# A hybrid decoder step on one core: the samples' rows between out-projection and experts, and the end of the last expert pair

## The reference, cut to what matters

```python
n = rmsnorm(h, norm_mix);  u = n @ w_in              # z | xBC | dt | q | k | v
y_ssd = ssd_branch(...)                               # conv, SiLU, Mamba-2 scan, gate, grouped norm
o     = dilated attention, merged, rmsnorm
h = h + concat(y_ssd, o) @ w_out                      # out-projection
x = rmsnorm(h, norm_ffn)
logits = x @ router_w + router_b                      # 32 experts
top_val, top_idx = top_k(logits, 4); gates = softmax(top_val)
for every token and each of its 4 experts e:
    hcat = x @ w1[e] + b1[e]                          # 1024 -> 2048
    g = min(glu, 7) * sigmoid(1.702 * min(glu, 7)) * (clip(lin, -7, 7) + 1)
    h += gate * (g @ w2[e] + b2[e])                   # 1024 -> 1024
y = rmsnorm(h, norm_final)
```

## Time and profile before

| what | value |
|---|---|
| median of 3 runs | 1234.51 us (1234.47 to 1235.19) |
| the profiled execution in all | 1238.29 us |
| its span | 1236.5 us |
| PE, DVE, ACT, POOL busy | 1155.0, 364.6, 230.2, 55.2 us |
| read from HBM, over the span | 455.82 MB, 375 GB/s |
| loads of experts, time from issue to landing | 37 to 39 us |

### The profile page before, as it was taken

One profiled execution on the slowest core, in us unless ns is written; L12 is line 12 of the kernel. 1 busy time (PEld: TensorE's weight loads), 2 busy tenths in 40 slices (PEclk: granted clock), 3 DMA queues, 4 the chain that ended last, 5 costly groups with the idle time before them and its releaser, 6 DMA issues.

```text
span 1236.5 us, 15869 instructions
## 1 busy us (share of the span) xinstructions
PE 1155.0 (93%) x6400; PEld 527.0 (43%) x6400; DVE 364.6 (29%) x749; ACT 230.2 (19%) x464; POOL 55.2 (4%) x49
## 2 busy tenths in 40 slices
PE   9999999899999999999989898989898989898897
PEld 7777666435443443434333332424242323232332
DVE  2467336764512130221213030303021121212122
ACT  2013453624501101111010101010111011010103
POOL 0000033530000000000000000000000000000000
PEclk9999999999899999999999999999999999999999
DMA  9677567479599999999999999999999999999996
GB/s 292 206 259 250 201 198 283 139 274 416 241 427 426 429 426 429 427 429 428 429 427 429 427 429 428 429 427 429 427 429 428 429 429 428 429 427 429 427 427 252
DMA packets 64368, 463.58 MB, mean 375 GB/s; under 512 B 7704, under 2 KB 25268, under 8 KB 38380
## 3 DMA queue, kind: packets, MB, share of 16 engines
q1 hardware_dynamic: 62206, 459.02, 90.2%
q10 hardware_dynamic: 1582, 2.22, 0.5%
q0 software_dynamic: 544, 1.84, 0.4%
HBM read 455.82 MB, written 7.24 MB: 375 GB/s over the span
## 4 chain that ended last, share of the span: by engine, by line
PE 57%; DMA 37%; DVE 2%; ACT 2%; issue 2%; SPq 0%; POOL 0%; ACTq 0%; DVEq 0%; POOLq 0%
DMA ring<-in_w 34%; PE ps L2399 21%; PE ps L1883 10%; PE ps L2423 5%; DMA own<-in_w 3%; PE ps L2331 2%; PE ps L2323 2%; PE ps L2291 2%; PE ps L2325 1%; PE ps L2168 1%; PE ps L1925 1%; PE ps L2342 1%; PE ps L2385 1%; PE ps L2210 1%; PE ps L1959 1%
## 5 line engine op out<-in xcount | busy, mean ns | idle before, releaser
L2399 PE MATMUL ps<-ring,own 128*64 128x512 f32 x1456 | 326.9, 595 | 29.6 <-DMA ring<-in_w 29.6
L1728 DVE TENSOR_SCALAR own<-ps 128x512 f32<-128x512 f32 x32 | 22.1, 692 | 678.9 <-PE ps L2399 678.7
L2399 PEld LDWEIGHTS ps<-ring,own 128*64 128x64 f32 x1456 | 104.1, 137 | 235.0 <-issue 178.9
L2423 PE MATMUL ps<-ring,own 128*64 128x512 f32 x592 | 133.5, 594 | 14.1 <-ACT own L1130 13.9
L2399 PE MATMUL ps<-own 128*64 128x512 f32 x592 | 134.1, 594 | 11.4 <-DMA own<-in_w 11.4
L1883 PE MATMUL ps<-own,ring 128*128 128x288 f32 x512 | 129.9, 409 | 0.0
L1883 PEld LDWEIGHTS ps<-own,ring 128*128 128x128 f32 x512 | 95.1, 190 | 28.8 <-issue 4.4
L2423 PE MATMUL ps<-own 128*64 128x512 f32 x432 | 98.4, 595 | 8.3 <-ACT own L1130 7.0
L2399 PEld LDWEIGHTS ps<-own 128*64 128x64 f32 x592 | 43.1, 137 | 94.7 <-issue 84.5
L2423 PEld LDWEIGHTS ps<-ring,own 128*64 128x64 f32 x592 | 44.1, 137 | 90.0 <-issue 70.3
L1130 ACT ACTIVATE own<-ps 64x512 f32<-64x512 f32 x60 | 35.5, 592 | 245.2 <-PE ps L2423 244.4
(11 more groups left out here) (378 smaller groups left out, 985.9 us busy)
## 6 DMA issues: line engine op xcount, KB each, us to landing
ring<-in_w SPq DMA_DIRECT2D x128, 2048.0 KB, 38.5
own<-in_w SPq DMA_DIRECT2D x63, 2048.0 KB, 37.4
ring<-in_w_in SPq DMA_DIRECT2D x16, 1024.0 KB, 7.8
ring<-in_cache_win_k SPq DMA_DIRECT2D x8, 1024.0 KB, 5.5
ring<-in_cache_win_v SPq DMA_DIRECT2D x8, 1024.0 KB, 4.8
ring<-in_w_out SPq DMA_DIRECT2D x6, 1024.0 KB, 10.9
ring<-in_state_ssm SPq DMA_DIRECT2D x8, 512.0 KB, 6.9
out_ssm_sample<-ring SPq DMA_DIRECT2D x8, 512.0 KB, 8.9
```

Source lines behind the costliest of these rows:

```text
L1728: nc.vector.tensor_scalar(xg_o, hid[:, 0], LIMIT, None, ALU.min).then_inc(sem("glu_ready"), 1)
L2399: last = nc.tensor.matmul(ps[C * half:C * half + C, 1 + m, :], xT[:, k, C * u:C * u + C], rows[:, D * half + 512 * m:D * half + 512 * m + ...
L2423: last = nc.tensor.matmul(ps[C * half:C * half + C, 4, :], gT[:, (k % 4) * P + C * (k // 4):(k % 4) * P + C * (k // 4) + C], rows[:, 512 * ...
```

## The change

- Between out-projection and experts, the samples: their three bf16 parts are now made right after their norm, ahead of the norm of tile 1, into `first_parts` (the room of `gT`, not yet in use). `first_places` writes the samples' selection three times, into 96 bf16 rows `S1s`. `first_samples` gathers them with eight bf16 products of 96 rows in place of `gather_tile(2, 1)`, in one go, after the turn of tile 1's second half; the openings follow the first half of tile 1's router instead of standing ahead of it. Tile 0's gather is cut after its first column block instead of in the middle. Later, ACT copies `first_parts` to `sample_parts`. `XN_PARTS` becomes 15.
- The end: in the last pair `second` of the first expert opens tile 1's banks at step 0, and tile 2's at step 4, where the second expert's turn now stands too; its columns go to a buffer of their own, `gT_last`. On ACT the copy of the first expert's rows (`closing_rows(pt, 0)`) comes after those columns and the last sums. After the second expert PE adds tile 1's first rows before it waits for the second rows, then tile 0's, tile 2's first, and the rest.
- The last units: 9 and 10 are loaded in two halves each, 11 in four quarters, each with a semaphore, and `second` waits for a piece when it comes to it.

```diff
+        S1s = sub(r_xbcP, 2 * 2 * C, C).bitcast(BF16)
+        first_parts = gT.bitcast(BF16)
-        XN_PARTS = 14
+        XN_PARTS = 15
+        gT_last = sub(r_xnT, D + TOK, 512)
+        END_ROWS = {9: (0, 2), 10: (0, 2), 11: (0, 1, 2, 3)}
+        def end_full(n, row):
+            return unit_full(n % UNITS) if row == 0 else sem(f"end_rows{n}_{row}")
...
@@ SP, last pair
-                if n < PER_PAIR - 1:
+                if n not in END_ROWS:
                     unit_load(NE - 2, n)
-            (two halves of the last unit, the second with sem("end_rows"))
+                    continue
+                of, _, j = pair_unit(n)
+                for row, end in zip(END_ROWS[n], END_ROWS[n][1:] + (W2_ROWS,)):
+                    sp.dma_start(unit(n % UNITS)[:, D * row:D * end], w2[NE - 2 + of, j][:, D * row:D * end]).then_inc(end_full(n, row), 16)
...
@@ ACT
+            act.wait_ge(sem("mixT_ps"), len(MIX_TURNS))
+            act.wait_ge(sem("xn_ready"), 2)
+            nc.scalar.activation(samples[NS:2 * NS], samples[0:NS], ACT.Copy)
+            rounded(samples[2 * NS:3 * NS], samples[0:NS], 2, 0)
+            rounded(first_parts[0:96], samples[0:96], 3, 0)
+            rounded(first_parts[NS:2 * NS], samples[NS:2 * NS], 4, 1)
+            rounded(first_parts[2 * NS:3 * NS], samples[2 * NS:3 * NS], 5, 1)
+            rounded(first_parts[2 * NS:3 * NS], samples[2 * NS:3 * NS], 6, 2)
             norm_tile(1, 2)
             normed_tile(1, 2)
             gate_exp(1, 2)
...
             act.wait_ge(sem("xT_ps"), 2)
-            nc.scalar.activation(samples[NS:2 * NS], samples[0:NS], ACT.Copy)
-            rounded(samples[2 * NS:3 * NS], samples[0:NS], 3, 0)
-            rounded(sample_parts[0:96], samples[0:96], 4, 0)
+            rounded(sample_parts[0:96], first_parts[0:96], 8, 0)
             for c in range(2):
-                rounded(token_parts[c][0], xn[:, c, :], 5 + c, 0)
-            rounded(sample_parts[NS:2 * NS], samples[NS:2 * NS], 7, 1)
-            rounded(sample_parts[2 * NS:3 * NS], samples[2 * NS:3 * NS], 8, 1)
-            rounded(sample_parts[2 * NS:3 * NS], samples[2 * NS:3 * NS], 9, 4)
+                rounded(token_parts[c][0], xn[:, c, :], 9 + c, 0)
...
@@ ACT, closing_turn
                 sums_to_banks(1)
-                closing_rows(pt, 0)
-                hidden_columns(2 * pt + 1)
+                hidden_columns(2 * pt + 1, gT_last)
                 act.wait_ge(sem("turned_ps"), 5)
                 sums_to_banks(2)
+                closing_rows(pt, 0)
...
@@ DVE, first_places
+                targets = [S1s[NS * r:NS * r + NS] for r in range(3)] if c == 2 else [S1[:, c]]
+                for to in targets:
+                    last = (the selection, built into `to`)
+                last.then_inc(sem("S_ready"), 1)
...
@@ DVE
+            left_over(xn[0:96, 2, :], first_parts[0:96], 4)
             add_mixed(1, 0)
+            dve.wait_ge(sem("xn_left"), 1)
+            left_over(xn[64:96, 2, :], first_parts[64:96], 6)
             tokens_to_lanes(1, 0, 4)
             add_mixed(1, 1)
             tokens_to_lanes(1, 1, 5)
...
@@ PE
+            def first_samples():
+                pe.wait_ge(sem("xn_ready"), 7)
+                pe.wait_ge(sem("S_ready"), 2)
+                for k in range(KT):
+                    nc.tensor.matmul(ps[:, FIRST_BANKS[k // 4], P * (k % 4):P * (k % 4) + P], first_parts[0:96, lane_columns(k)], S1s[0:96], start=False, stop=False)
...
+            half_scored()
             pe.wait_ge(zeroed, 6)
             pe.wait_ge(sem("b1_parts"), 6)
             for bank in FIRST_BANKS:
                 nc.tensor.matmul(ps[:, bank, :], zeros, b1p[0:1, 0:512], start=True, stop=False)
-            gather_tile(2, 1, (0,))
-            half_scored()
             pe.wait_ge(sem("h_mixed"), 5)
             h_turn(1, 1)
-            gather_tile(2, 1, (1,))
+            first_samples()
             pe.wait_ge(sem("xnT_dve"), 13)
             router(1, range(4, KT))
-            gather_tile(0, 0, (0,))
+            first_tile(0, 0, 1, range(1))
             router_sum(1, 2)
-            gather_tile(0, 0, (1,))
+            first_tile(0, 0, 1, range(1, KT))
             prefix(1, 2)
...
-            gather_tile(1, 2)
+            first_tile(1, 2, 8, range(KT))
...
@@ PE, second
-                        if ending and n == PER_PAIR - 1 and k % W2_ROWS == 2:
-                            pe.wait_ge(sem("end_rows"), 16)
+                        if ending and k % W2_ROWS in END_ROWS.get(n, ())[1:]:
+                            pe.wait_ge(end_full(n, k % W2_ROWS), 16)
...
-                    second(pt, 0, first, {4: open_rest} if closing else {})
-                    pe.wait_ge(sem("gT_ready"), 2 * pt + 1)
-                    hidden_turn(pt, 1)
+                    second(pt, 0, first, {0: open_next, 4: open_last_and_turn} if closing else {})
+                    if not closing:
+                        pe.wait_ge(sem("gT_ready"), 2 * pt + 1)
+                        hidden_turn(pt, 1)
...
+            pe.wait_ge(sem("read_act"), 4)
+            add_closing(1, 0)
             pe.wait_ge(sem("ysb_ready"), more * (4 * PASS_STEP * PAIRS) + (4 * PAIRS + 1))
+            add_closing(0, 1).then_inc(sem("comb_ps"), 1)
+            pe.wait_ge(sem("read_act"), 5)
+            add_closing(2, 0)
+            for c in range(1, 3):
                 add_closing(c, 1).then_inc(sem("comb_ps"), 1)
```

More of the change, by code:

```diff
@@ L1083, in _, with rounded @@
             nc.scalar.activation(stat[:, 61:62], stat[:, 60:61], ACT.Sqrt)
+            def rounded(to, source, rounds, left):
+                act.wait_ge(sem("xn_ready"), rounds)
+                if left:
+                    act.wait_ge(sem("xn_left"), left)
+                nc.scalar.activation(to, source, ACT.Copy).then_inc(sem("xn_ready"), 1)
+            samples = xn[:, 2, :]
+            act.wait_ge(sem("mixT_ps"), len(MIX_TURNS))
[6 more added lines that the diff above has]
+            rounded(first_parts[2 * NS:3 * NS], samples[2 * NS:3 * NS], 6, 2)
             norm_tile(1, 2)
@@ L1739, in _ @@
             dve.wait_ge(sem("gate_ready"), 3)
-            for rows, tiles in ((P, slice(0, 2)), (NS, slice(2, 3))):
-                _, weights, _, s1, s2 = pair_views(0, rows, tiles, S1)
-                nc.vector.tensor_tensor(s2, s1, weights, ALU.mult).then_inc(sem("S_ready"), 1)
+            _, weights, _, s1, s2 = pair_views(0, P, slice(0, 2), S1)
+            nc.vector.tensor_tensor(s2, s1, weights, ALU.mult).then_inc(sem("S_ready"), 1)
+            nc.vector.tensor_tensor(S2[0:NS, 2].rearrange("p (u c) -> p u c", u=2), S1s[0:NS].rearrange("p (u c) -> p u c", u=2),
+                                    gate[0:NS, 2, 0:2].unsqueeze(2).broadcast_to([NS, 2, C]), ALU.mult).then_inc(sem("S_ready"), 1)
             for r in range(1, 3):
@@ L2202, in lane_columns, with first_tile @@
                 return slice(start, start + W1_ROWS * (P - 1) + 1, W1_ROWS)
-            def gather_tile(c, s, halves=(0, 1)):
-                n = ROWS[c]
-                pe.wait_ge(sem("xn_ready"), s + 1)
+            def first_tile(c, s, ready, ks):
+                pe.wait_ge(sem("xn_ready"), ready)
                 pe.wait_ge(sem("S_ready"), s + 1)
-                for half in halves:
-                    for j in range(4):
-                        last = nc.tensor.matmul(ps[:, FIRST_BANKS[half], P * j:P * j + P], xn[0:n, c, lane_columns(4 * half + j)], S1[0:n, c, :], start=False, stop=(c == 1 and j == 3))
-                    if c == 1:
+                for k in ks:
+                    last = nc.tensor.matmul(ps[:, FIRST_BANKS[k // 4], P * (k % 4):P * (k % 4) + P], xn[:, c, lane_columns(k)], S1[:, c, :], start=False, stop=(c == 1 and k % 4 == 3))
+                    if c == 1 and k % 4 == 3:
                         last.then_inc(sem("xT_ps"), 1)
+            def first_samples():
[3 more added lines that the diff above has]
+                    nc.tensor.matmul(ps[:, FIRST_BANKS[k // 4], P * (k % 4):P * (k % 4) + P], first_parts[0:96, lane_columns(k)], S1s[0:96], start=False, stop=False)
             natural = list(range(12))
```

47 lines of the change are left out of this document (17 added, 30 removed).

## The result

The change made the kernel slower: 1240.86 us, median of 7 (1239.35 to 1241.37), against 1235.72 us (1234.47 to 1237.49) of the kernel before on the same chip; ratio 1.0032, interval 1.0017 to 1.0047. The profiled execution of after took 1241.37 us with a span of 1239.6. The forecast was 1229.2, and the range ended at 1234.4.

The account below looks back on a forecast made before the run. The expert weights' DMA stream sets the pace over most of the span, with gains only before and after it; head 5.1 plus tail 0.2 makes 5.3 us off 1234.51, so 1229.2 us, range 1227.0 to 1234.4.

Parts of the forecast that it names:

- The ground: Head to last landing: each microsecond the first expert starts earlier moves the whole weights' stream, and so the end, forward.
- A: Head: the granted clock stays high; gain 3.7 to 6.6 us, 5.1 taken, 1229.2 us with the tail; chance 0.50.
- B: Head: the clock falls all the same; gain 0.7 to 1.4 us, 1.1 taken, 1233.2 us with the tail; chance 0.40.
- the 32-row lots: Head: the samples' 32-row products ahead of the clock's fall become 96-row matmuls, an argument for A; no size of its own.
- The size of the head: Head up to the first expert: 5.1 us gained, the middle of A's 3.7 to 6.6.
- A's far end: Head: the high clock holds to the end of the low stretch, a gain of 6.6 us.
- C: Head: roundings and subtractions on ACT and DVE at twice their price come 5.6 us late for PE; 1238.8 us, chance 0.06.
- The tail: From the ninth unit to the end: together a gain of 0.2 us, bounds 0.5 gain and 0.2 loss.
- The first openings: Tail: two openings (0.5 us) move to where PE idled 1.30 us, but wait for DVE's read, so hidden or not.
- the 0.19 us of the wait for unit 10: Tail: PE's 0.19 us wait goes, since the turn comes ahead of the last half of unit 9.
- the four records: Tail after the second expert: four closing-sum records (0.94 us) move under a 0.76 us wait; 0.15 to 0.75 us kept.
- D: Tail: each of eight load pieces costs 0.4 us more than its bytes, 3.2 us using up slack and gain; 1235, chance 0.04.

Follow-up runs that it names:

- the shifted after: Changed kernel with three of six warm-up products written as 24 small ones, so its expert loop begins at 4080, not 4044: 1234.61 us, ratio 0.9989.
- past the limit: Kernel before with all six warm-up products written as 48 small ones, so its loop spans 4133 to 5863: 1246.30 us, ratio 1.0087.
- the control: Kernel before with the same 36 added warm-up instructions, loop from 4097 to 5827: 1237.26 us, ratio 1.0016.
- the two halves: Kernel before with only PE's new head order (1236.87 us, ratio 1.0003), and with only the new bf16 sample parts in the old order (1236.14 us, ratio 0.9993).
- three more traces of the old head: Kernel before with 36 or 72 more instructions ahead of the loop, or eleven idle products each turn: head stretch 14.1, 14.3 and 13.0 us.

## Why the prediction was wrong

- **The ground: "Each microsecond by which this start comes forward moves the whole stream forward, up to the last landing".** This step failed. The stream did start with the first unit's release, 5.1 us earlier, as the prediction's last paragraph asked, but it did not keep its pace: 830.6 us for 822.8. The prediction counted instructions that went away on PE only as time at the head; that 17 fewer of them move the code behind them was not in it. No rival covered it. The term that is missing is worth 7.6 to 7.9 us on the stream, and in the totals 6.3 us (after against the shifted after, two sessions) to 9.0 (past the limit against the control, 2.2 of it ahead of the loop). Against the kernel before on the same chip the forecast was 10.4 us off: the stream 7.8, the head 3.0, the tail 0.6, which is 1.0 too much and within the scatter.
- **The clock (A against B).** A's mechanism was right: clock 1.00 from 304 to 318, the expert at 312.76, inside "311 to 313". The reason, "the 32-row lots", is borne out by the two halves, as a likelihood, and for the lots as they were: rows, type and number changed together.
- **The size of the head.** 5.1 came out at the first landing of the profiled execution, but that it hit the middle of A is luck: the stretch itself shrank by 6.2 (17.8 to 11.6), near A's far end of 6.6, and the mixer ended 1.8 later. 2.1 us is what the totals show, and 1.5 to 2.7 what three more traces of the old head leave to win. The prediction subtracted the low stretch of a 1238.29 us execution from a median of 1234.51. It named that doubt and used it only against 6.6; by its own words on B, a usual run with little of the low level would have given 1.3, so the truth lay between A and B. This term was mis-sized: 5.1 for a measured 2.1 (0.2 to 3.3).
- **ACT and DVE (C).** Right: the roundings cost nothing. ACT's last of them ended near 302.3 for a start at 304.40 (2.1 us of slack for the forecast 2.2).
- **The tail.** A gain of 0.2 with a loss of at most 0.2 was forecast; it was a loss of 0.4. From the ninth unit to the first closing sums 9.85 us came out (9.36 before, "9.0 to 9.5" forecast). Two sizes were off. The first openings were "hidden or not"; they are not, they wait for VectorE past the landing, so nothing but the 0.19 us of the wait for unit 10 pays for the 0.59 by which the wait for ACT grew (0.17 to 0.76). And the four records moved under the last 0.76 bring 0.1 us at the last tile, not 0.15 to 0.75, since ACT and DVE still follow tile by tile.
- **The pieces (D).** Right that they cost nothing: PE waits for none. In the shifted after they flow at 416 GB/s at 1214 to 1216, as the earlier trace rows had promised, and the last three units take 15.0 us for 14.75, not the 18.4 estimated from the Trainium skill ("DMA: Bandwidth & Descriptors", section Bandwidth). The 203 GB/s of after at 1218 to 1220 are not theirs: the run past the limit has the same without pieces.

## What to carry to other kernels

Where a long hand-written loop fills most of an engine's instruction memory, an edit anywhere ahead of it can cost more than it wins: compare the row for instruction packets and the "issue" waits at the loop's first line before and after every change, and move the loop by a few instructions that compute nothing if they have grown. On a stream that fills the transfer engines, code is paid for there, and most on the engines that carry it, not in the stall. And a low clock that one profiled execution shows should be priced from several.

## What the runs showed of the hardware

- PE keeps code over turns of a loop: 1730 to 1774 instructions (111 to 114 KB) ran from about 460 to 1170 us without a fetch, as long as they lay in 7 blocks of 256; 1730 in 8 blocks were fetched again in each turn, at 36 more packets in all (nine in each of four turns), a stall at the loop's start (two waits of 2.1 and 5.1 us in after) and 7.6 to 7.8 us on the weights' stream.
- The Trainium skill, "Runtime: NRT & Kernel Launch", section Instruction fetch mechanics, gives PE an instruction memory of 128 KiB, filled in blocks of 16 KiB, and has a stall where a taken branch leaves what is there. The blocks and the stall agree with these traces. The 128 KiB are eight blocks, yet a loop in eight was fetched again. The two fit together if the block behind the loop is fetched while the loop's last block runs: then a loop in seven leaves room for it, and a loop in eight doesn't and costs nine packets a turn, the number that after and the run past the limit show. This is worked out from counts and was not tried by a run of its own. What the section says of two lines (with the 32 KiB of other engines) and of prefetch that gains nothing from locality does not hold for PE here, since 7 blocks stayed for some 700 us.
- Fetches that take 0.34% of the transfer engines' time made the stream 0.9% longer, as the sixteen parts of a unit drifted apart, from 2.1 us between the first and the last to 10.0 (a share of about 0.50 over the last 8 us).
- Sixteen f32 records on 32 rows were followed by the low clock in four of five profiled executions, eight bf16 products on 96 rows in none of eight, with PE idle for longer in the latter. Rows, type and number of the records were not changed one by one.
